# A trunk step of two layers: where the final norm is applied, and who stores its output

## The chip, the cores and the metric

The kernel runs on one core of one Trainium2 chip. The time is the device time in microseconds (us). All times in the profile are us from the start of the span unless marked ns. The engines are TensorE (PE; its weight loads are PEld), VectorE (DVE), ScalarE (ACT), GpSimd (POOL) and SyncE (SP, which only issues DMAs here).

## The reference

One inference step of a decoder trunk of depth 2, width 1024, float32, for 512 prompt tokens and 8 x 4 sample tokens (32). Each layer is an attention and mLSTM mixer with an output projection, then a convolutional feed-forward part with a down projection, each added to the residual stream. At the end stands the final norm, which is what the change touches:

```
def rmsnorm(x, g):
    xf = x.astype(F32)
    y = xf * lax.rsqrt(jnp.mean(xf * xf, axis=-1, keepdims=True) + EPS)
    return (y * g.astype(F32)).astype(x.dtype)
...
    y_prompt = rmsnorm(xp, final_g)
    y_sample = rmsnorm(xs, final_g)
```

## The kernel before

Activations are kept transposed: `xT` is [128 partitions, 8 chunks, 544 tokens], the width of 1024 being split into eight chunks of 128 (`KC` = 8). The tokens are 512 prompt ones (`SEQ`) and 32 sample ones (`TS`), 544 (`TT`) in all. Big products are made of three products of rounded parts each (line 1237 for the up projection, line 1263 for the down projection).

The instructions of each engine stand in one block, in program order, and the engines are tied by semaphores alone. There is no planner: the order is written out by hand. In the last down projection (`down(2, NG, last=True)`, lines 1251 to 1279) TensorE makes chunk 0 to 7 of the output, 12 matmul pairs each. VectorE adds each chunk to the residual stream (`residual`, lines 2259 to 2270; the last instruction, line 2270, signals `y_add`). ScalarE squares the chunk (line 1332) into one of two halves of `sq`. Two chunks later TensorE sums the squares over the partitions (`norm_sum`, lines 638 to 646): four matmuls with a 128x32 block of ones, each for a quarter of the 544 tokens (136), put the sums of quarter q in partitions 32q to 32q+31 of one PSUM bank. Between the chunks TensorE also turns the last rows of the convolution history (`tail_rows`, line 1248), which ScalarE copies (line 1663) and GpSimd stores (lines 2515 and 2516).

After chunk 7 the norm is finished in this order. VectorE adds epsilon (line 1695), ScalarE takes the root (line 1337), VectorE inverts 136 columns (line 1697), TensorE spreads the four quarters over all partitions (`spread`, lines 648 to 654), ScalarE copies the part of the sample tokens (line 1339). VectorE makes `xnT`: the sample tokens by two products (lines 2381 and 2383) and the prompt tokens by eight `scaled` (line 1703), each a chunk times the gain times the spread inverse root. TensorE then transposes `xnT` back to rows of tokens in ten tiles of 128 tokens by 512 columns (32 tokens in the last two), four transposes each, into four PSUM banks in turn (lines 1311 to 1320). The first half of a row needs chunks 0 to 3, the second chunks 4 to 7. ScalarE copies each tile to `ybuf` (lines 1670 to 1673), and GpSimd stores it (lines 2520 to 2526).

SyncE's queue carries only loads; its last ones are the last rows of the down weights (line 628), long before this point. GpSimd's queue carries all stores. `in_norm(S, m, k)` is the k-th increment of semaphore S in norm number m; the final norm is m = 4.

Of the kernel before, what the change touches and what calls it, by code (L numbers as in the profile page):

```python
# [13 lines left out]
D = 1024  # L14
SEQ = 512
# [110 lines left out]
def trunk_program(nc, A, O):  # L126
# [10 lines left out]
    with ctx:  # L137
# [213 lines left out]
        final_tr, final_copy = sig("final_transposed", 10), sig("final_copied", 10)  # L351
# [167 lines left out]
        def _(sp):  # L519
# [22 lines left out]
            for L in range(DEPTH):  # L542
# [6 lines left out]
                def load(stage, i, copies, j=0):  # L549

                    s = i % NSLAB
                    sp.wait_ge(slab_out[s], L * uses[s] + j + (first_use[stage, s] + i // NSLAB) + 1)
                    for dst, src in copies:
                        sp.dma_start(dst, src).then_inc(slab_in[s], 16)
# [73 lines left out]
                load("ffn", 16, down_copies(lambda k: slice(4 * NG + k, 4 * NG + k + 1), 1))  # L628


        @block.tensor
        def _(pe):
# [72 lines left out]
            for L in range(DEPTH):  # L705
# [544 lines left out]

                def down(n_k, g=0, last=False):
# [4 lines left out]
                    for c in range(8):  # L1256
# [11 lines left out]
                        if last:  # L1268
                            if c == 0:
                                pe.wait_ge(y_add.sem, y_add.at(8 * g, L))  # L1270
                            if c < 6:
                                tail_rows(c)
                            if c >= 2:
                                norm_sum(2 * L + 2, c - 2)
                    pe.drain().then_inc(slab_out[1], 1)
                    if last:
                        norm_sum(2 * L + 2, KC - 2)
                        norm_sum(2 * L + 2, KC - 1)
                        spread(2 * L + 2)
# [30 lines left out]

            for n in range(10):
                t, hf = n // 2, n % 2
                M = 128 if t < 4 else TS
                if n < 2:
                    pe.wait_ge(n_dve.sem, in_norm(n_dve, 2 * DEPTH, 4 * hf + 6))
                if n >= 4:
                    pe.wait_ge(final_copy.sem, final_copy.at(n - 3))
                for k in range(4):
                    ins = tr(ps[n % 4][0:M, 128 * k:128 * k + 128], xnT[:, 4 * hf + k, 128 * t:128 * t + M], ident)
                ins.then_inc(final_tr.sem, 1)  # L1320

        @block.scalar
        def _(act):
# [54 lines left out]
            for L in range(DEPTH):  # L1378
# [289 lines left out]
                root(2 * L + 2)  # L1668

            for n in range(10):  # L1670
                M = 128 if n < 8 else TS
                act.wait_ge(final_tr.sem, final_tr.at(n + 1))
                A_(ybuf[0:M, n, :], ps[n % 4][0:M, :], ACT.Copy).then_inc(final_copy.sem, 1)


        @block.vector
        def _(dve):
# [91 lines left out]
            for L in range(DEPTH):  # L1769
# [606 lines left out]
                inverse_root(2 * L + 2)  # L2376

            m = 2 * DEPTH
            dve.wait_ge(n_act.sem, in_norm(n_act, m, KC + 2))
            d = xnT[:, :, SEQ:TT]  # L2380
            tt(d, xT[:, :, SEQ:TT], bc(rd, 1, KC), ALU.mult)
            drain()
            tt(d, d, bc(colsB[:, 88:96], 2, TS), ALU.mult)
            drain()
            for k in range(KC):
                scaled(m, k, colsB[:, 88 + k:89 + k])
# [3 lines left out]
        def _(pool):  # L2390
# [35 lines left out]
            for L in range(DEPTH):  # L2426
# [86 lines left out]
                decode_scaled(2 * L + 1, 24)  # L2513
                pool.wait_ge(ul_c.sem, ul_c.at(6, L))
# [5 lines left out]
            for n in range(10):  # L2520
                t, hf = n // 2, n % 2
                pool.wait_ge(final_copy.sem, final_copy.at(n + 1))
                dst = y_p[0, 128 * t:128 * t + 128, 512 * hf:512 * hf + 512] if t < 4 else \
                    y_s.rearrange("b t d -> (b t) d")[:, 512 * hf:512 * hf + 512]
                pool.dma_start(dst, ybuf[0:128 if t < 4 else TS, n, :]).then_inc(stored, 16)
            pool.wait_ge(stored, DEPTH * ST_ALL + 160)
# [31 lines left out]
```

## Time and profile before

| | |
|---|---|
| median of 3 runs | 1839.16 us (1837.89 to 1844.75) |
| profiled execution | 1831.91 us |
| its span | 1830.1 us |
| instructions in the span | 37052 |
| TensorE busy | 1698.8 us, 93% |
| VectorE busy | 919.4 us, 50% |
| ScalarE busy | 610.7 us, 33% |
| GpSimd busy | 187.5 us, 10% |
| mean granted TensorE clock | 0.950 |

The span runs from the first to the last instruction of the profiled execution. A granted clock of 1.00 is 2.4 GHz, of 0.50 1.2 GHz. Busy shares are means over the span; the stretch that the change touches is the last 45 us or so, and is read from its own rows.

### The profile page before, as it was taken

To read this page: it belongs to the slowest core of one execution; us is meant where nothing else is said; L and a number is where in the kernel's file an instruction comes from. 1 tells how busy PE (TensorE), PEld (TensorE's weight loads), DVE (VectorE), ACT (ScalarE), POOL (GpSimd) and SP (SyncE) were. 2 spreads that over 40 slices of the span, in tenths; PEclk is the share of its full clock that TensorE was granted. 3 is DMA by queue.
4 is the path that set the end of the run, shared out by engine and by line. 5 is a ranking of instruction groups with operands and counts; after the bars stand their busy time and mean duration, and the time that the engine had idled before them with its cause. 6 is when DMAs were issued, how large, how long until landed. Compare 5 with 4: busy or idle time off the path is not lost.

```text
span 1830.1 us, 37052 instructions
## 1 busy us (share of the span) xinstructions
PE 1698.8 (93%) x14719; PEld 1526.7 (83%) x14719; DVE 919.4 (50%) x2374; ACT 610.7 (33%) x1165; POOL 187.5 (10%) x304
## 2 busy tenths in 40 slices
PE   5899998977989999999989999898798999999996
PEld 4799965545989999999989997645598999999995
DVE  2534434646365645546463343474545554654644
ACT  2332225634142323323152212463333332422413
POOL 1001003432000000000000100153200000000001
PEclk9899988988989999999999997898898999999998
DMA  8335278369322222221133535634861222221201
GB/s 297 118 99 181 78 273 261 115 225 200 82 76 65 92 93 93 93 92 47 49 89 90 179 102 186 221 105 137 217 114 47 92 93 93 93 92 47 93 24 54
DMA packets 157903, 219.42 MB, mean 120 GB/s; under 512 B 11722, under 2 KB 116490, under 8 KB 157548
## 3 DMA queue, kind: packets, MB, share of 16 engines
q1 hardware_dynamic: 150096, 199.22, 34.7%
q0 software_dynamic: 7648, 17.94, 3.9%
q8 instruction: 116, 1.90, 0.4%
q14 instruction: 43, 0.35, 0.1%
HBM read 200.45 MB, written 16.68 MB: 119 GB/s over the span
## 4 chain that ended last, share of the span: by engine, by line
PE 85%; DVE 5%; ACT 3%; SPq 2%; issue 2%; DMA 1%; POOL 1%; DVEq 1%; ACTq 0%
PE ps L1237 28%; PE ps L1263 15%; PE ps L809 13%; PE ps L1197 6%; PE ps L683 2%; PE ps L920 2%; PE ps L935 2%; PE ps L854 2%; PE ps L890 1%; PE ps L795 1%; PE ps L804 1%; PE ps L803 1%; SPq L546 1%; PE ps L1217 1%; PE ps L870 1%
## 5 line engine op out<-in xcount | busy, mean ns | idle before, releaser
L1237 PE MATMUL ps<-work_r,big_r 128*128 128x272 f32 x1344 | 279.2, 289 | 1.4 <-ACT work L1622 0.3
L1237 PE MATMUL ps<-work_r,slab_r 128*128 128x272 f32 x1344 | 278.5, 288 | 0.0
L1237 PE MATMUL ps<-xnT_r,big_r 128*128 128x272 f32 x1344 | 276.4, 287 | 0.0
L1237 PEld LDWEIGHTS ps<-work_r,big_r 128*128 128x128 f32 x1344 | 210.2, 188 | 3.9 <-issue 3.9
L809 PE MATMUL ps<-slab_r,work_r 128*128 128x256 f32 (+1 forms) x976 | 213.3, 285 | 0.0
L1237 PEld LDWEIGHTS ps<-xnT_r,big_r 128*128 128x128 f32 x1344 | 211.7, 188 | 0.0
L1237 PEld LDWEIGHTS ps<-work_r,slab_r 128*128 128x128 f32 x1344 | 210.5, 188 | 0.0
L1727 DVE TENSOR_TENSOR slab_r<-slab,big_r 128x2048 fp32r<-128x2048 f32 (+1 forms) x84 | 170.2, 2036 | 49.5 <-ACT big_r L1606 44.1
L809 PEld LDWEIGHTS ps<-slab_r,work_r 128*128 128x128 f32 x976 | 163.4, 191 | 2.7 <-issue 2.5
L1625 ACT ACTIVATE big<-big,work 128x560 f32<-128x560 f32 x44 | 33.7, 765 | 372.1 <-DVE big L2321 372.1
L1263 PE MATMUL ps<-side_r,big_r 128*128 128x272 f32 x704 | 148.3, 292 | 4.9 <-DVE big_r L1727 4.9
L1263 PE MATMUL ps<-big_r 128*128 128x272 f32 x704 | 146.3, 289 | 0.0
L1263 PE MATMUL ps<-side_r,slab_r 128*128 128x272 f32 x704 | 145.9, 289 | 0.0
L2265 DVE TENSOR_TENSOR work<-ps,modT 128x32 f32<-128x32 f32 x112 | 21.5, 192 | 241.6 <-PE ps L1263 181.2
L2431 POOL DMA_DIRECT2D out<-work x32 | 18.3, 578 | 1064.8 <-ACT work L1663 810.9
L1263 PEld LDWEIGHTS ps<-side_r,big_r 128*128 128x128 f32 x704 | 111.0, 190 | 7.7 <-DVE big_r L1727 5.4
L1263 PEld LDWEIGHTS ps<-big_r 128*128 128x128 f32 x704 | 111.5, 190 | 0.0
L1263 PEld LDWEIGHTS ps<-side_r,slab_r 128*128 128x128 f32 x704 | 111.0, 190 | 0.0
L1606 ACT ACTIVATE big_r<-slab 128x2048 fp32r<-128x2048 f32 x44 | 84.3, 1916 | 48.4 <-PE ps L1237 48.4
L809 PE MATMUL ps<-work_r 128*128 128x256 f32 (+1 forms) x336 | 96.3, 287 | 0.0
L809 PE MATMUL ps<-work_r,xnT_r 128*128 128x256 f32 (+1 forms) x336 | 94.1, 280 | 0.0
L809 PE MATMUL ps<-slab_r,xnT_r 128*128 128x256 f32 x320 | 90.8, 284 | 0.0
(446 smaller groups left out, 3204.9 us busy)
## 6 DMA issues: line engine op xcount, KB each, us to landing
slab<-in_w_mod SPq DMA_DIRECT2D x23, 2048.0 KB, 9.0
slab<-in_w_up SPq DMA_DIRECT2D x44, 1024.0 KB, 7.5
slab<-in_w_in SPq DMA_DIRECT2D x20, 1024.0 KB, 5.9
slab<-in_w_down SPq DMA_DIRECT2D x20, 1024.0 KB, 6.0
slab<-in_cache_cmp_kv SPq DMA_DIRECT2D x128, 128.0 KB, 2.0
slab<-in_cache_sel_kv SPq DMA_DIRECT2D x96, 128.0 KB, 2.0
big<-in_cache_win_kv SPq DMA_DIRECT2D x16, 512.0 KB, 5.2
out<-big POOLq DMA_DIRECT2D x16, 448.0 KB
```

The lines of the kernel that those rows point to most:

```text
L683: ins = mm(bank[32 * q:32 * q + 32, 0:128], cT[:, k, :], wv[:, k, 128 * q:128 * q + 128], start=k == 0, stop=k == KC - 1, tile_position=(0 ...
L809: ins = mm(ps[n % 4][:, 0:cw], x, fr(wt[:, k, :]), start=k == 0 and m == 0, stop=k == KC - 1 and m == 2)
L854: mm(ps[2 * (s % 2) + k][:, 0:nk], proj[h_, t, 128 * g:128 * g + 128], proj[h_, 0:t + 1, c:c + 128], start=True, stop=True).then_inc(a_s.s ...
L920: ins = tr(ps[4 + k][:, 128 * i:128 * i + 128], Pq[u % 6][:, 128 * i:128 * i + 128], ident)
L935: ins = mm(ps[6][64 * k:64 * k + 64, 128 * i:SEQ], proj[:, i, c + 64 * k:c + 64 * k + 64], PT[:, n % 2, k, 512 * i:384 * i + SEQ], start=b ...
L1197: ins = mm(ps[2 * (c % 3) + b][:, 0:HALF], wt, fr(x[:, k, HALF * b:HALF * b + HALF]), start=k == 0 and n == 0, stop=k == KC - 1 and n == 2)
L1237: ins = mm(ps[2 * half + b][:, 0:HALF], wt, fr(x[:, k, HALF * b:HALF * b + HALF]), start=k == 0 and n == 0, stop=k == KC - 1 and n == 2)
L1263: ins = mm(ps[bank + b][:, 0:HALF], wt, fr(x[:, k, HALF * b:HALF * b + HALF]), start=k == 0 and n == 0, stop=k == n_k - 1 and n == 2)
L1606: A_(fr(hiU[:, q % 2, :, :, :]), src[:, :, :, cc:cc + 128], ACT.Copy).then_inc(w_hi.sem, 1)
L1625: A_(cv[:, s, 0:UPW - 2], cv[:, s, 0:UPW - 2], ACT.Silu, bias=cbias[:, s:s + 1]).then_inc(u_si.sem, 1)
L1727: return tt(fr(dst), dst, fr(hi).bitcast(F), ALU.subtract)
L2265: tt(tmp.rearrange("p (b t) -> p b t", b=NB), hi[:, SEQ - HALF:HALF].rearrange("p (b t) -> p b t", b=NB), bc(gs, 2, NT), ALU.mult)
```

## The change

The final norm is no longer applied ahead of the transposes. The gain is applied first: GpSimd multiplies chunks 0 to 5 with their column of the gain as each is added, ScalarE chunks 6 and 7 after its last square. The inverse root is applied when a transposed tile is copied out of PSUM, where a token is a partition and its factor a scalar of the partition. For that the sums of squares are made for blocks of 128 tokens (`token_sums`) and turned into columns by two transposes (`token_columns`); ScalarE takes the root of five columns and VectorE inverts them. The tiles are in another order (all first halves, then all second halves) and in other banks; the first is transposed between chunks 6 and 7, and three more before the last sums. VectorE copies the even tiles and ScalarE the odd ones. SyncE stores them in place of GpSimd. The norms inside the layers stay as they were.

```diff
+        FINAL = [(n % 5, n // 5, b) for n, b in enumerate((7, 4, 5, 0, 1, 2, 3, 7, 4, 5))]
+        y_out = ctx.enter_context(nc.semaphore("final_stored"))
...
         @block.sync
+            for n, (t, hf, _) in enumerate(FINAL):
+                if n % 2:
+                    sp.wait_ge(final_copy.sem, final_copy.at(n // 2 + 1))
+                else:
+                    sp.wait_ge(n_dve.sem, in_norm(n_dve, 2 * DEPTH, 3 + n // 2))
+                cols = slice(512 * hf, 512 * hf + 512)
+                if t < 4:
+                    sp.dma_start(y_p[0, 128 * t:128 * t + 128, cols], ybuf[:, n, :]).then_inc(y_out, 16)
+                else:
+                    sp.dma_start(y_s.rearrange("b t d -> (b t) d")[:, cols], ybuf[0:TS, n, :]).then_inc(y_out, 16)
+            sp.wait_ge(y_out, 160)
...
         @block.tensor
+                def token_sums(k):
+                    pe.wait_ge(n_act.sem, in_norm(n_act, 2 * DEPTH, k + 1))
+                    for q in range(4):
+                        mm(ps[6][32 * q:32 * q + 32, 0:128], ones[:, 0:32], sq[:, k % 2, 128 * q:128 * q + 128], start=k == 0,
+                           stop=k == KC - 1, tile_position=(0, 32 * q), skip_group_check=True)
+                    mm(ps[6][0:TS, 128:128 + TS], ones[:, 0:TS], sq[:, k % 2, SEQ:TT], start=False, stop=k == KC - 1,
+                       tile_position=(0, 0), skip_group_check=True).then_inc(n_pe.sem, 1)
+
+                def token_columns():
+                    pe.wait_ge(n_dve.sem, in_norm(n_dve, 2 * DEPTH, 1))
+                    tr(ps[6][:, 256:384], rstd[:, 0:128], ident)
+                    tr(ps[6][0:TS, 384:384 + TS], rstd[0:TS, 128:128 + TS], idn(TS)).then_inc(n_pe.sem, 1)
+
+                def final_tile(n):
+                    t, hf, bank = FINAL[n]
+                    M = 128 if t < 4 else TS
+                    pe.wait_ge(n_pool.sem, in_norm(n_pool, 2 * DEPTH, (4, 6)[hf]))
+                    if hf:
+                        pe.wait_ge(n_act.sem, in_norm(n_act, 2 * DEPTH, KC + 2))
+                    if n == 7:
+                        pe.wait_ge(n_dve.sem, in_norm(n_dve, 2 * DEPTH, 3))
+                    if n == 8:
+                        pe.wait_ge(final_copy.sem, final_copy.at(1))
+                    if n == 9:
+                        pe.wait_ge(n_dve.sem, in_norm(n_dve, 2 * DEPTH, 4))
+                    for k in range(4):
+                        ins = tr(ps[bank][0:M, 128 * k:128 * k + 128], xnT[:, 4 * hf + k, 128 * t:128 * t + M], ident)
+                    ins.then_inc(final_tr.sem, 1)
...
-                            if c >= 2:
+                            if c >= 2 and L + 1 < DEPTH:
                                 norm_sum(2 * L + 2, c - 2)
+                            elif c >= 2:
+                                token_sums(c - 2)
+                            if c == 6 and L + 1 == DEPTH:
+                                final_tile(0)
                     pe.drain().then_inc(slab_out[1], 1)
-                    if last:
+                    if last and L + 1 == DEPTH:
+                        pe.wait_ge(ul_c.sem, ul_c.at(6, L))
+                        token_sums(KC - 2)
+                        final_tile(1)
+                        final_tile(2)
+                        pe.wait_ge(y_add.sem, y_add.at(8 * g + 7, L))
+                        final_tile(3)
+                        token_sums(KC - 1)
+                        final_tile(4)
+                        token_columns()
+                        pe.wait_ge(y_add.sem, y_add.at(8 * g + 8, L))
+                        for n in range(5, 10):
+                            final_tile(n)
+                    elif last:
...
         @block.scalar
+                    if L + 1 == DEPTH and c == KC - 1:
+                        for k in (KC - 2, KC - 1):
+                            A_(xnT[:, k, :], xT[:, k, :], ACT.Copy, scale=colsB[:, 88 + k:89 + k]).then_inc(n_act.sem, 1)
...
+            act.wait_ge(n_pe.sem, in_norm(n_pe, 2 * DEPTH, KC + 1))
+            A_(rstd[:, 160:164], ps[6][:, 256:384].rearrange("p (t n) -> p t n", t=4)[:, :, 0], ACT.Sqrt)
+            A_(rstd[0:TS, 164:165], ps[6][0:TS, 384:385], ACT.Sqrt).then_inc(n_act.sem, 1)
+            act.wait_ge(n_dve.sem, in_norm(n_dve, 2 * DEPTH, 2))
+            for n, (t, hf, bank) in enumerate(FINAL):
+                if n % 2:
+                    act.wait_ge(final_tr.sem, final_tr.at(n + 1))
+                    r = slice(0, 128) if t < 4 else slice(0, TS)
+                    A_(ybuf[r, n, :], ps[bank][r, :], ACT.Copy, scale=rstd[r, 160 + t:161 + t]).then_inc(final_copy.sem, 1)
...
         @block.vector
-            dve.wait_ge(n_act.sem, in_norm(n_act, m, KC + 2))
-            d = xnT[:, :, SEQ:TT]
-            tt(d, xT[:, :, SEQ:TT], bc(rd, 1, KC), ALU.mult)
-            drain()
-            tt(d, d, bc(colsB[:, 88:96], 2, TS), ALU.mult)
-            drain()
-            for k in range(KC):
-                scaled(m, k, colsB[:, 88 + k:89 + k])
+            dve.wait_ge(n_pe.sem, in_norm(n_pe, m, KC))
+            ts_(rstd[:, 0:128], ps[6][:, 0:128], 1.0 / D, EPS, ALU.mult, ALU.add)
+            ts_(rstd[0:TS, 128:128 + TS], ps[6][0:TS, 128:128 + TS], 1.0 / D, EPS, ALU.mult, ALU.add).then_inc(n_dve.sem, 1)
+            dve.wait_ge(n_act.sem, in_norm(n_act, m, KC + 3))
+            V.reciprocal(rstd[:, 160:164], rstd[:, 160:164])
+            V.reciprocal(rstd[0:TS, 164:165], rstd[0:TS, 164:165]).then_inc(n_dve.sem, 1)
             drain()
+            for n, (t, hf, bank) in enumerate(FINAL):
+                if n % 2 == 0:
+                    dve.wait_ge(final_tr.sem, final_tr.at(n + 1))
+                    r = slice(0, 128) if t < 4 else slice(0, TS)
+                    ts_(ybuf[r, n, :], ps[bank][r, :], rstd[r, 160 + t:161 + t], None, ALU.mult).then_inc(n_dve.sem, 1)
...
         @block.gpsimd
+                if L + 1 == DEPTH:
+                    for c in range(KC - 2):
+                        pool.wait_ge(y_add.sem, y_add.at(8 * NG + c + 1, L))
+                        nc.gpsimd.tensor_scalar(xnT[:, c, :], xT[:, c, :], colsB[:, 88 + c:89 + c], 1.0, ALU.mult,
+                                                ALU.mult).then_inc(n_pool.sem, 1)
                 pool.wait_ge(ul_c.sem, ul_c.at(6, L))
                 put(p_conv[L].rearrange("o j f -> (o j) f"), ulrow[0:2, :])
                 put(s_conv[L].rearrange("b j f -> (b j) f"), ulrow[2:18, :])
```

The old loops of final transposes, copies and stores (lines 1311 to 1320, 1670 to 1673, 2520 to 2525) go, and so do `root`, `inverse_root` and `spread` for the final norm.

## Rows read from the trace of the kernel before

**Rows 1.** The page, part 4: the chain that ended last, by engine.

```profile
PE 85%; DVE 5%; ACT 3%; SPq 2%; issue 2%; DMA 1%; POOL 1%; DVEq 1%; ACTq 0%
```

**Rows 2.** Chain of waits, 1775 to 1831, in time order: start, length, what.

```profile
1798.98 0.44 PE ps L1248 x4
...
1804.13 1.72 PE ps L1263 x12
...
1807.15 0.67 ACT big L1332
...
1807.86 0.48 PE ps L642 x8
...
1811.27 0.18 PE ps L654 x2
...
1818.11 3.69 PE ps L1319 x16
```

**Rows 3.** Timeline of VectorE there: start, length, instruction, idle before and its releaser.

```profile
1790.32 0.19 DVE L2270 TENSOR_TENSOR xT<-xT,work 128x32 f32<-128x32 f32 x1
...
1806.92 0.19 DVE L2270 TENSOR_TENSOR xT<-xT,work 128x32 f32<-128x32 f32 x1
1808.36 0.30 DVE L1695 TENSOR_SCALAR rstd<-ps 128x136 f32<-128x136 f32 x1 [1.25 <-PE ps L642]
1809.05 1.00 DVE L1697 RECIPROCAL rstd<-rstd 128x136 f32<-128x136 f32 x1 [0.38 <-ACT rstd L1337]
...
1812.69 5.36 DVE L1703 SCALAR_TENSOR_TENSOR xnT<-xT,colsB,ps 128x512 f32<-128x512 f32 x8
```

**Rows 4.** Timeline of ScalarE there.

```profile
1808.70 0.32 ACT L1337 ACTIVATE rstd<-rstd 128x136 f32<-128x136 f32 x1 [0.89 <-DVE rstd L1695]
...
1821.82 2.98 ACT L1673 ACTIVATE big<-ps 128x512 f32<-128x512 f32 x6 [0.25 <-PE ps L1319]
```

**Rows 5.** Timeline of GpSimd there.

```profile
1817.52 0.57 POOL L2525 DMA_DIRECT2D out<-big  x1 [14.01 <-ACT big L1673]
...
1822.71 3.15 POOL L2525 DMA_DIRECT2D out<-big  x6 [0.31 <-ACT big L1673]
```

**Rows 6.** Half microseconds: busy by engine; last come clock, DMA share, GB/s.

```profile
1766.50:1767.00 0.50, 0.50 (x6) 0.50 (x5) 0.42 (x2) 0.00 (x0) 0.00 (x0) 1.00 0.65 74
...
1811.50:1812.00 0.50, 0.00 (x0) 0.00 (x0) 0.30 (x1) 0.16 (x1) 0.00 (x0) 0.50 0.00 0
1818.50:1819.00 0.50, 0.50 (x4) 0.50 (x3) 0.00 (x0) 0.00 (x0) 0.00 (x0) 0.50 0.70 270
...
1821.50:1822.00 0.50, 0.50 (x6) 0.50 (x5) 0.00 (x0) 0.25 (x2) 0.19 (x2) 0.85 0.88 328
...
1828.00:1828.50 0.50, 0.00 (x0) 0.00 (x0) 0.00 (x0) 0.00 (x0) 0.00 (x0) 0.97 0.00 0
```

**Rows 7.** Groups, shapes kept apart: busy, mean ns of one, idle before.

```profile
L2468 POOL TENSOR_SCALAR xnT<-xnT,rstd,gates 128x512 f32<-128x512 f32 x20 | 15.2, 772 | 3.1 <-DVE rstd L2024 3.1
...
L2453 POOL TENSOR_TENSOR big<-big,rows_bc 128x2048 f32<-128x2048 f32 x2 | 9.1, 4547 | 121.1 <-ACT big L1423 121.1
...
L2097 DVE COPY work<-ps 128x512 f32<-128x512 f32 x24 | 16.6, 691 | 21.0 <-PE ps L1033 20.8
```

**Rows 8.** Timeline of SyncE's DMA issues.

```profile
136.52 8.72 SPq L547 DMA_DIRECT2D slab<-in_cache_cmp_kv  x8
...
380.40 1.76 SPq L599 DMA_DIRECT2D big<-in_cache_win_kv  x4
...
1765.93 0.83 SPq L554 DMA_DIRECT2D slab<-in_w_down  x2
```

**Rows 9.** Stretches of 4 us while modulation weights are loaded, as rows 6.

```profile
226.00:230.00 4.00, 3.89 (x21) 2.65 (x22) 3.71 (x9) 1.41 (x2) 0.96 (x1) 1.00 0.89 286
230.00:234.00 4.00, 2.62 (x7) 1.35 (x5) 2.12 (x5) 2.71 (x11) 0.00 (x0) 0.63 1.05 393
```

**Rows 10.** Timeline of TensorE in the tail.

```profile
1815.47 1.12 PE L1319 MATMUL ps<-shape_constants,xnT 128*128 128x128 f32 x4 [4.04 <-DVE xnT L1703]
```

More of the change, by code:

```diff
@@ L350, in trunk_program @@
         c_in = ctx.enter_context(nc.semaphore("conditions_and_pages_loaded"))
-        final_tr, final_copy = sig("final_transposed", 10), sig("final_copied", 10)
+        final_tr, final_copy = sig("final_transposed", 10), sig("final_copied_act", 5)
+        FINAL = [(n % 5, n // 5, b) for n, b in enumerate((7, 4, 5, 0, 1, 2, 3, 7, 4, 5))]
+        y_out = ctx.enter_context(nc.semaphore("final_stored"))
         stored = ctx.enter_context(nc.semaphore("outputs_stored"))
@@ L1309, in _ @@
                 down(2, NG, last=True)
[L1311 to L1320, printed above, removed]
         @block.scalar
@@ L1667, in _ @@
                         split_in(0, L + 1)
[L1668 to L1673, printed above, removed]
+                    if L + 1 == DEPTH and c == KC - 1:
+                        for k in (KC - 2, KC - 1):
+                            A_(xnT[:, k, :], xT[:, k, :], ACT.Copy, scale=colsB[:, 88 + k:89 + k]).then_inc(n_act.sem, 1)
+                if L + 1 < DEPTH:
+                    root(2 * L + 2)
+            act.wait_ge(n_pe.sem, in_norm(n_pe, 2 * DEPTH, KC + 1))
[7 more added lines that the diff above has]
+                    A_(ybuf[r, n, :], ps[bank][r, :], ACT.Copy, scale=rstd[r, 160 + t:161 + t]).then_inc(final_copy.sem, 1)
         @block.vector
@@ L2375, in _ @@
                 add_y(NG, 0)
-                inverse_root(2 * L + 2)
+                if L + 1 < DEPTH:
+                    inverse_root(2 * L + 2)
             m = 2 * DEPTH
-            dve.wait_ge(n_act.sem, in_norm(n_act, m, KC + 2))
-            d = xnT[:, :, SEQ:TT]
-            tt(d, xT[:, :, SEQ:TT], bc(rd, 1, KC), ALU.mult)
-            drain()
-            tt(d, d, bc(colsB[:, 88:96], 2, TS), ALU.mult)
-            drain()
-            for k in range(KC):
-                scaled(m, k, colsB[:, 88 + k:89 + k])
+            dve.wait_ge(n_pe.sem, in_norm(n_pe, m, KC))
[4 more added lines that the diff above has]
+            V.reciprocal(rstd[0:TS, 164:165], rstd[0:TS, 164:165]).then_inc(n_dve.sem, 1)
+            drain()
+            for n, (t, hf, bank) in enumerate(FINAL):
[3 more added lines that the diff above has]
+                    ts_(ybuf[r, n, :], ps[bank][r, :], rstd[r, 160 + t:161 + t], None, ALU.mult).then_inc(n_dve.sem, 1)
         @block.gpsimd
@@ L2519, in _ @@
                 assert n_st[0] == ST_ALL, (n_st[0], ST_ALL)
[L2520 to L2526, printed above, removed]
+            pool.wait_ge(stored, DEPTH * ST_ALL)
 _INS = ["x_prompt", "x_sample", "cache_cmp_kv", "cache_sel_kv", "cache_win_kv", "state_mlstm_C", "state_mlstm_n",
```

## The prediction

> **What bounds the kernel now.** I read the page's split of the chain of waits first: 85% of it is TensorE [rows 1], so over the trunk only TensorE's work counts. The change leaves the trunk alone and rewrites what follows the last down projection, so I then read the chain in order of time from there. The matmuls of chunk 7 end at 1805.85 [rows 2] and the last residual addition at 1807.11 [rows 3]. From there to the end of the span, 1830.1, are 23.0 us, and hardly any of it is matmul work: square 0.67 and sums 0.48 [rows 2], variance 0.30, a 1.00 reciprocal over 136 columns [rows 3], the spread over the partitions, decode products, eight scalings in 5.36 [rows 3], transposes (16 of them in 3.69 [rows 2]), ScalarE's copies, ten stores in turn on GpSimd's queue [rows 4, 5], and their landing. Every step waits for the one before. TensorE's granted clock falls to 0.50 (1.2 GHz) in this tail, with TensorE idle for up to 4.04 at a stretch, and comes back to 1.00 (2.4 GHz) between 1821.5 and 1822 [rows 6, 10]. The tail is a latency chain and then a store phase, and the change rewrites both.
>
> **The change part by part**, on the profile's own clock (span 1830.1, execution 1831.91, so 1.8 lie around the span).
>
> *Delay ahead of the last addition.* In chunks 2 to 7 each sum of squares becomes four 128-column matmuls and one 32-column one in place of four 136-column ones. An f32 matmul is two records in the trace, so eight become 8 + 2. The two extra cost between nothing and 0.18, the price of the spread's two 32-column records [rows 2], which load full-width weights; the eight cost 0.48, 0.06 each [rows 2], and each becomes narrower. I take 0.06 in all, the nearer row being the same operation's, six times: 0.35 (bounds 0 and 1.1). After chunk 6's matmuls TensorE also transposes the first final tile, ahead of chunk 7's. Four transposes cost 0.44 where the clock is full and 3.69/4 = 0.92 where it is half [rows 2]; here it is full: 0.44. Together the last addition moves by 0.8, to 1807.9.
>
> That tile waits for GpSimd's fourth scaling, and chunk 7's matmuls stand behind the wait. GpSimd took 0.77 for such an operation on 128x512 and 4.55 for a product of two tensors of 2048 columns [rows 7], so 128x544 is 0.8, at most 1.2. The additions that release it end from 1790.51 on, 2.37 apart in the mean [rows 3], so it keeps pace; the fourth is scaled near 1798.5, and TensorE asks near 1804.5. The wait costs nothing below some 3.4 an operation, and all six scalings lie beside matmuls. Behind them on GpSimd are the last two convolution-state stores, which move back by about 1; nothing reads them and they land before the final stores begin.
>
> *The norm.* From the addition at 1807.9: square with its hop 0.7, to 1808.6. TensorE meanwhile does chunk 6's sums and three tiles (0.45 + 3 x 0.44 after 1806.65) and is just free; chunk 7's sums to 1809.15. VectorE's variance is two operations, 0.30 [rows 3] and 0.2 for the small one: 1809.65; the fifth tile hides in that. Two transposes make it columns, 0.25: 1809.9. ScalarE takes two small roots, each under the 0.32 of the root over 136 columns [rows 4], overlapping: 0.35, to 1810.25. Ahead of them it has the scalings of chunks 6 and 7, as wide as its square, so 0.67 each [rows 2], from 1808.6: done by 1809.95, with the columns. No table is loaded for the root, as none is before the one at 1808.70 [rows 4]. VectorE inverts 128x4 and 32x1, each like its smallest operation, 0.19 [rows 3]: 0.3 overlapping, to 1810.55 (bound above 1.0, the old reciprocal). So the long reciprocal, the spread, the decode products and the eight scalings go, and from last addition to inverse it is 2.65.
>
> *Evictions and the last five tiles.* Five tiles lie in PSUM by then; the others are transposed from 1809.9 at 0.44, paced by banks that come free, until about 1813. VectorE evicts even tiles in 0.69 [rows 7], ScalarE odd ones in 0.50 (six in 2.98 [rows 4]) with the multiplication inside, side by side. The first tile is ready at 1811.25, the last near 1814. What is late next is the stores.
>
> *Stores.* They move from GpSimd, 3.15/6 = 0.53 an issue [rows 5], to SyncE. SyncE issued 512 KB of window rows in 0.44 (four in 1.76), but eight pages in 8.72, whose issues carry a register load each [rows 8]. Ours have constant addresses like the former: 0.44, so the ten take 4.4 and do not bind. From issue to first data a load on this queue took 1.0 (issued at 1765.93, data between 1766.5 and 1767 [rows 6, 8]), and so did a GpSimd store (1817.52, data after 1818.5 [rows 5, 6]). Data flow from 1812.3. The output is 544 rows of 1024 f32, 2.23 MB. On this queue loads ran at 286 to 393 GB/s when many were under way [rows 9]; the old stores made 328 in a busy half microsecond [rows 6]. Bounds 7.8 and 5.7; I take 360 GB/s, between the rows, 6.2: 1818.5. From the last data, 1828.0, to the end of the span took 2.1 [rows 6]. New end 1820.6: 9.5 less.
>
> Two rules of the Trainium skill speak to this, and no number above uses them. "TensorE: Matmul & The Clock Gate", Part 4 on PE-mode transpose, says the full clock does not engage for transposes, since they don't count as busy. This trace shows the opposite: from 1818.11 TensorE runs nothing but transposes [rows 2], and the clock rises to 1.00 within them [rows 6]. By the row it stays full in the new tail; by the rule the last tiles run at half, 0.92 each, and the sum is some 0.5 worse. "DMA: Bandwidth & Descriptors", Latency and other measured facts, puts a hardware queue's first byte 0.4 ahead of GpSimd's; the rows show 1.0 for both, and by the rule the sum would be 0.4 better.
>
> The median of the runs shown is 1839.16, 7.3 above the profiled execution. I take the saving off it: 1839.16 - 9.5 = 1829.7.
>
> **The rivals.**
> 1. *SyncE's issues pace the stores.* For it: eight page issues in 8.72 [rows 8]. Against: the 0.44 of the window loads beside them. At 1.05 the tenth issue starts at 1811.3 + 9.5 = 1820.8 and the span ends 1.0 + 0.2 + 2.1 later, 1824.1: saving 6.0, time 1833.2. A store rate of 286 costs 1.6 more than the forecast and joins this case.
> 2. *The clock falls in the new tail.* For it: it fell by 1811.5 in the old one [rows 6]. Against: there TensorE had little to do, here tiles fill its waits. Columns and three last tiles at half cost 0.3 + 0.7: 1830.7.
> 3. *Nothing of the delay shows:* extra matmuls are free and stores run at 393 GB/s: 0.35 + 0.5 more saved, 1828.8.
> 4. *Slower.* No store stands on SyncE's queue anywhere in the trace, only loads. If 2 KB rows written from it ran slowly, the store phase would give all back. It breaks even where 2.23 MB take 6.2 + 9.5 = 15.7, 142 GB/s; at 85 GB/s they take 26.2, and the time is 1849.7. For it: only that it is unseen. Against: loads of this queue run as fast as GpSimd's stores did [rows 6, 9].
>
> **How the numbers follow.** Forecast 0.51 (own range 1828.0 to 1831.5), rival 1 0.24, rival 2 0.10, rival 3 0.12, rival 4 0.03. A measurement of this kernel tells a change of about 0.5%, 9.2 us, from none. The forecast is on that edge: 0.33 of its 0.51 lies beyond it, and with rival 3 and a little of the others faster has 0.48. Slower is rival 4, 0.03; the rest, 0.49, is within 0.5%. The range goes from rival 3 less 2.3 (the three runs of before spread over 6.9, so a median may move by some 2) to rival 1 plus 1.8: 1826.5 to 1835.0.
>
> **What would show it.** The last residual's end some 0.8 later; the inverse 2.65 after it; evictions on both engines in step; SyncE's ten issues at 0.44; data without gaps for about 6.2; the granted clock at 1.00 until TensorE's last transpose; a span of 1820.6. I am wrong if issues are 1.0 apart, if the data phase passes 7.8, or if chunk 7's matmuls wait for GpSimd.

## The result and the profile after

The changed kernel takes 1826.05 us (median of 8 runs, 1823.34 to 1831.08). The kernel before, run again beside it, has a median of 1836.38 over its now 8 runs (1829.23 to 1844.75). The ratio is 0.9941, 95% interval 0.9923 to 0.9960: 10.3 us less by the medians. A second set of runs on one chip gave 1826.89 against 1836.98, ratio 0.9943 (0.9927 to 0.9960). The forecast was a saving of 9.5 us and a time of 1829.7, range 1826.5 to 1835.0. The measured time lies 0.45 us under the range.

The page of the changed kernel, its span and part 4:

```profile
span 1824.0 us, 37076 instructions
...
PE 86%; DVE 4%; ACT 3%; SPq 2%; issue 2%; DMA 1%; POOL 1%; DVEq 1%; ACTq 0%
```

The share of TensorE in the chain [rows 1] is up a point, as the tail around it is shorter. The chain of waits of the changed kernel from chunk 6 on (start, length, what), against [rows 2]:

```profile
1806.68 1.70 PE ps L1309 x12
1808.38 0.35 PE ps L1269 x8
1808.73 0.04 PE ps L1271 x2
1808.77 0.59 PE ps L1294 x4
1809.36 1.50 PE ps L1309 x12
...
1811.26 0.27 issue
...
1811.97 1.46 PE ps L1294 x12
1813.43 0.36 PE ps L1269 x8
...
1815.36 2.71 DVE big L2452 x4
```

The timeline of VectorE. Its first line is the start of the product for the last chunk of the hidden layer of the feed-forward part; its second line answers to the last addition in [rows 3], the 0.18 and the 0.12 to the reciprocal of 1.00 there:

```profile
1790.46 0.44 DVE L2390 TENSOR_TENSOR big<-ps,big 128x272 f32<-128x272 f32 x1 [2.89 <-PE ps L1251]
...
1811.95 0.19 DVE L2331 TENSOR_TENSOR xT<-xT,work 128x32 f32<-128x32 f32 x1
1813.87 0.29 DVE L2442 TENSOR_SCALAR rstd<-ps 128x128 f32<-128x128 f32 x1 [1.72 <-PE ps L1271]
...
1815.04 0.18 DVE L2445 RECIPROCAL rstd<-rstd 128x4 f32<-128x4 f32 x1 [0.80 <-ACT rstd L1728]
1815.14 0.12 DVE L2446 RECIPROCAL rstd<-rstd 32x1 f32<-32x1 f32 x1
1815.35 3.37 DVE L2452 TENSOR_SCALAR big<-ps,rstd 128x512 f32<-128x512 f32 x5
```

ScalarE and GpSimd in the same stretch (the last square, the two scalings, the five copies; and the fourth of GpSimd's scalings):

```profile
1812.18 0.66 ACT L1384 ACTIVATE big<-xT 128x544 f32<-128x544 f32 x1 [1.83 <-DVE xT L2331]
1812.74 1.37 ACT L1722 ACTIVATE xnT<-xT,colsB 128x544 f32<-128x544 f32 x2
...
1815.29 3.17 ACT L1734 ACTIVATE big<-ps,rstd 128x512 f32<-128x512 f32 x5 [0.28 <-DVE rstd L2446]
```

```profile
1802.37 0.72 POOL L2583 TENSOR_SCALAR xnT<-xT,colsB 128x544 f32<-128x544 f32 x1 [1.82 <-DVE xT L2331]
```

SyncE's ten final issues, in place of GpSimd's [rows 5]:

```profile
1816.13 1.81 SPq L639 DMA_DIRECT2D out<-big  x4
1817.99 0.55 SPq L641 DMA_DIRECT2D out<-big  x1
1818.58 2.29 SPq L639 DMA_DIRECT2D out<-big  x4
1820.91 0.67 SPq L641 DMA_DIRECT2D out<-big  x1
```

Half microseconds of the changed kernel, with the columns of [rows 6]:

```profile
1816.50:1817.00 0.50, 0.50 (x7) 0.50 (x6) 0.50 (x2) 0.50 (x2) 0.00 (x0) 1.00 0.06 25
1817.00:1817.50 0.50, 0.50 (x7) 0.43 (x5) 0.50 (x2) 0.50 (x2) 0.00 (x0) 1.00 1.01 377
...
1820.50:1821.00 0.50, 0.00 (x0) 0.00 (x0) 0.00 (x0) 0.00 (x0) 0.00 (x0) 1.00 1.05 397
...
1822.50:1823.00 0.50, 0.00 (x0) 0.00 (x0) 0.00 (x0) 0.00 (x0) 0.00 (x0) 0.50 1.00 320
1823.00:1823.50 0.50, 0.00 (x0) 0.00 (x0) 0.00 (x0) 0.00 (x0) 0.00 (x0) 0.50 0.18 62
1823.50:1824.00 0.50, 0.00 (x0) 0.00 (x0) 0.00 (x0) 0.00 (x0) 0.00 (x0) 0.50 0.00 0
```

I measure the tail from the end of the last residual addition to the end of the span, because it doesn't move with what the trunk did before: 1807.11 to 1830.1 is 23.0 before, 1812.14 to 1824.0 is 11.9 after. So the tail lost 11.1 us. Read in the same four pieces as the prediction, whose values for the kernel before come from half microseconds:

| piece | before | predicted | after |
|---|---|---|---|
| last addition to first store's issue | 10.4 | 3.4 | 4.0 |
| issue to first data | 1.0 | 1.0 | 0.8 |
| first to last data | 9.5 | 6.2 | 6.3 |
| last data to end of the span | 2.1 | 2.1 | 0.8 |

Data fill the DMA engines without a gap from 1817.0 to 1823.0, at shares of 0.92 to 1.07. Nine of these twelve half microseconds have 365 to 397 GB/s, three have 275 to 320. The last data are seen at 1823.2. TensorE's last transpose ends at 1817.75, and the granted clock is still 1.00 in the slice from 1820.5; that from 1822.5 has 0.50.

The spans of the two profiled executions differ by only 6.1, though the tail alone is 11.1 shorter. The rest is the trunk. VectorE's product for the last hidden chunk starts at 1784.40 in the profile of before and at 1790.46 in this one, with the same instructions ahead of it.

### The profile page after: what moved, and what is told of

It reads as the page before. It is cut to its first block, busy times and chain, and to the rows that moved or that the text cites. A ratio compares the mean times of both kernels' runs of the same rounds, so it can differ in the third digit from the quotient of the medians.

```text
span 1824.0 us, 37076 instructions
## 1 busy us (share of the span) xinstructions
PE 1700.2 (93%) x14727; PEld 1528.8 (84%) x14727; DVE 916.1 (50%) x2371; ACT 609.5 (33%) x1162; POOL 185.6 (10%) x300
## 4 chain that ended last, share of the span: by engine, by line
PE 86%; DVE 4%; ACT 3%; SPq 2%; issue 2%; DMA 1%; POOL 1%; DVEq 1%; ACTq 0%
PE ps L1251 28%; PE ps L1309 15%; PE ps L823 13%; PE ps L1211 6%; PE ps L697 3%; PE ps L934 2%; PE ps L949 2%; PE ps L868 2%; PE ps L1231 2%; PE ps L904 1%; PE ps L809 1%; PE ps L818 1%; SPq L548 1%; PE ps L817 1%; DMA work<-in_x_sample 1%
```

## The experiments

All numbers below are tails as defined above, read from each kernel's own profile; the ratio is of timed runs to the kernel before. "To the addition" is the time from the start of VectorE's last hidden product (first line of the VectorE fence above) to the end of the last addition.

| kernel | tail | to the addition | ratio (95%) |
|---|---|---|---|
| before | 22.99 | 22.71 | 1 |
| changed | 11.86 | 21.68 | 0.9941 (0.9923 to 0.9960) |
| changed, again | 11.88 | 23.23 | 0.9943 (0.9927 to 0.9960) |
| gpsimd_stores | 14.60 | 23.24 | 0.9971 (0.9951 to 0.9992) |
| scalar_copies | 11.72 | 23.25 | 0.9939 (0.9918 to 0.9960) |
| both_undone | 14.15 | 23.25 | 0.9951 (0.9933 to 0.9970) |
| before_sync_stores | 20.91 | 22.73 | 0.9996 (0.9981 to 1.0012) |
| before_kept_busy | 25.75 | 21.17 | 1.0018 (1.0000 to 1.0036) |
| before_kept_busy_short | 22.13 | 22.73 | 0.9984 (0.9969 to 0.9999) |
| gpsimd_all_eight | 11.87 | 23.26 | 0.9941 (0.9923 to 0.9958) |
| sums_first | 11.48 | 23.24 | 0.9932 (0.9908 to 0.9956) |
| tile_behind | 11.54 | 22.85 | 0.9932 (0.9900 to 0.9964) |
| drain_last | 11.38 | 21.28 | 0.9925 (0.9906 to 0.9944) |
| half_stored | 10.27 | 23.26 | one run |

Two profiles of the changed kernel have tails of 11.86 and 11.88, and the span is shown to 0.1 us, so with SyncE's stores a tail tells a change of 0.1 to 0.2 us, where the timed ratio tells some 3 us. No kernel with GpSimd's stores was profiled twice; a difference of a few tenths between those is less sure.

### What of the change is worth what

**Stores back on GpSimd.**

```diff
-            for n, (t, hf, _) in enumerate(FINAL):      # in block.sync
...
+            for n, (t, hf, _) in enumerate(FINAL):      # at the end of block.gpsimd
+                ...
+                    pool.dma_start(y_p[0, 128 * t:128 * t + 128, cols], ybuf[:, n, :]).then_inc(y_out, 16)
```

> The changed kernel with the ten final stores back on GpSimd's queue, nothing else. I read the tail: from the end of the last residual addition to the end of the span, 23.0 us before, 11.9 after. Theory A: ten stores of 2.23 MB are bound by the DMA engines (share 1.0, some 380 GB/s) on either queue, and SyncE's queue only ends sooner (0.9 from last data to the end of the span after, 2.1 before): tail 13.1, i.e. +1.2. Rival B: the queue sets the store rate itself; GpSimd's stores had half microseconds at 0.47 to 0.7 of share before, so the data phase goes from 6.2 to 7.5 or more: tail 14.5 or more. Rival C: the queue is worth nothing, tail 11.9.

Measured: tail 14.60, 2.7 more than the changed kernel. Theory A's 13.1 falls and rival B's tail holds, though the data phase is 7.3 and not 7.5 or more. The sooner end that theory A named is in the 2.7 as well. GpSimd's first issues and half microseconds:

```profile
1819.25 2.17 POOL L2587 DMA_DIRECT2D out<-big  x4 [7.18 <-DVE big L2441]
```

```profile
1820.00:1820.50 0.50, 0.50 (x6) 0.29 (x3) 0.50 (x2) 0.50 (x1) 0.50 (x2) 1.00 0.27 106
...
1821.00:1821.50 0.50, 0.00 (x0) 0.00 (x0) 0.50 (x1) 0.32 (x1) 0.50 (x2) 1.00 0.61 213
...
1823.50:1824.00 0.50, 0.00 (x0) 0.00 (x0) 0.00 (x0) 0.00 (x0) 0.50 (x2) 0.50 0.86 205
...
1827.50:1828.00 0.50, 0.00 (x0) 0.00 (x0) 0.00 (x0) 0.00 (x0) 0.00 (x0) 0.50 0.05 16
```

The first issue comes 4.25 after the last addition (4.0 on SyncE), the first data 1.1 after it, the data end near 1827.7, 7.3 later (6.3 on SyncE), and the span 1.9 after that (0.8). Before 1826.5 the share is 0.61, 0.78 and twice 0.86 in four slices, where the changed kernel never falls under 0.92. So the queue counts at four places: 0.25, 0.25, 1.1 and 1.1.

**Copies by ScalarE alone.**

```diff
-                if n % 2:
+                if True:                                 # ScalarE copies all ten tiles
                     act.wait_ge(final_tr.sem, final_tr.at(n + 1))
...
-            for n, (t, hf, bank) in enumerate(FINAL):    # VectorE's copies
```

> The changed kernel with all ten copies out of PSUM on ScalarE, none on VectorE. Theory A (stores bound the end): ScalarE delivers a tile per 0.63, the DMA engines take 0.68 for one, so the last data move by under 0.3 and the tail stays 11.9 to 12.3. Rival B (copies bound the end once one engine makes them): ten copies at 0.63 plus a hop each for tiles 7 to 9, that now wait for a bank, end 3 us later and the tail is 13 or more.

Measured: tail 11.72, 0.14 less. ScalarE's copies, and the end of the data:

```profile
1817.73 5.81 ACT L1727 ACTIVATE big<-ps,rstd 128x512 f32<-128x512 f32 x10 [0.28 <-DVE rstd L2439]
```

```profile
1825.00:1825.50 0.50, 0.00 (x0) 0.00 (x0) 0.00 (x0) 0.00 (x0) 0.00 (x0) 0.50 0.78 234
1825.50:1826.00 0.50, 0.00 (x0) 0.00 (x0) 0.00 (x0) 0.00 (x0) 0.00 (x0) 0.50 0.00 0
```

Ten copies take 5.81, 0.58 apart, where ScalarE's five beside VectorE's are 0.63 apart, and the first store can go at 1818.45, 3.87 after the addition instead of 4.0. The tail lies 0.2 under theory A's range, but its mechanism holds and rival B falls: the stores take 6.2 and hide the copies. Sharing the copies between two engines, part of the change, gave nothing here.

**Both undone.** The edits of the two above together.

> The changed kernel with both undone: copies by ScalarE alone and stores on GpSimd's queue. What is left of the change is the norm behind the transposes with its gain by GpSimd. Theory A: the two add up to +1.2 to +1.6, tail 13.1 to 13.5; then 9.5 of the 11.1 us that the tail lost belong to the reordered norm. Rival B: the rest is worth under half, tail 17 or more.

```profile
1806.56 0.19 DVE L2316 TENSOR_TENSOR xT<-xT,work 128x32 f32<-128x32 f32 x1
```

Measured: the span is 1820.9, so the tail is 14.15. That is 0.65 over theory A's range, whose store term was 1.2 where gpsimd_stores has 2.7. Its main point stands: with GpSimd's stores and one copying engine the reordered norm brings the tail from 22.99 to 14.15, 8.8 of the 11.1 us. These 8.8 include the new order of the tiles and the clock that stays up; no run separates them. With the stores on GpSimd, ScalarE alone is 0.45 faster than the pair (14.15 against 14.60): the first issue comes 0.12 sooner and the data phase is some 6.9 in place of 7.3. Why it gains more there than the 0.14 with SyncE's stores stays open.

**Only the stores moved, in the kernel before.**

```diff
-                pool.wait_ge(final_copy.sem, final_copy.at(n + 1))
+                sp.wait_ge(final_copy.sem, final_copy.at(n + 1))
...
-                pool.dma_start(dst, ybuf[0:128 if t < 4 else TS, n, :]).then_inc(stored, 16)
+                sp.dma_start(dst, ybuf[0:128 if t < 4 else TS, n, :]).then_inc(y_out, 16)
```

> The kernel before with its ten final stores on SyncE's queue, nothing else. Theory A: the old tail is paced by transposes and ScalarE's copies up to 1824.8, so the queue gives only its sooner end, -1.2, and little by shorter issues: tail 21.4 to 22.0. Rival B: the queue's rate counts: tail 20.5 or less. Rival C: nothing, 23.0.

Measured: tail 20.91, 2.1 less. That is 0.5 under theory A's range and 0.4 over rival B's, so neither holds as stated; the timed ratio, 0.9996 (0.9981 to 1.0012), can't tell 2 us from nothing. The last copy ends 17.7 after the addition in both kernels. The last data come 2.1 after that copy in place of 3.1, and the span ends 1.1 after them in place of 2.2, both read in slices of 0.1 us. So the queue is worth 2.1 in the old order and 2.7 behind the reordered norm.

**GpSimd scaling all eight chunks.**

```diff
-                    for c in range(KC - 2):
+                    for c in range(KC):
...
-                        for k in (KC - 2, KC - 1):       # ScalarE's two scalings
-                            A_(xnT[:, k, :], xT[:, k, :], ACT.Copy, scale=colsB[:, 88 + k:89 + k]).then_inc(n_act.sem, 1)
```

> The changed kernel with GpSimd scaling all eight chunks and ScalarE none. Theory A: ScalarE's two scalings (1.37, ending 1814.11) are off the path, its roots wait for TensorE's columns until 1814.80; GpSimd would end chunk 7 at 0.75 after the last addition. The tail stays 11.9 within 0.2. Rival B: TensorE's second-half tiles wait for ScalarE's scalings now, and the tail shortens by 0.5 or more.

Measured: tail 11.87. Theory A holds, ScalarE's two scalings are hidden as the prediction had them.

### The clock in the old tail

```diff
+                def busy(n):
+                    for _ in range(n):
+                        mm(ps[4][:, 0:128], ident, ident, start=True, stop=True)
...
+                            busy(12)                     # 5 in the second kernel
                         spread(2 * L + 2)
+                            busy(30)                     # 13
...
+                if n == 0:
+                    busy(12)                             # 5
```

> The kernel before with 12 + 30 + 12 extra 128-column matmuls of the unit matrix into an unused bank, placed where TensorE idles in the tail (before the spread, behind it, behind the first tile). Theory A: the fall of the granted clock to 0.50 costs the old tail real time: its 16 chained transposes took 3.69 at half clock and would take 1.8 at full, so the tail goes from 23.0 to about 21, and that much of the change's gain is the clock. Rival B: the copies pace anyway and the clock is worth under 0.5: tail 22.5 or more. If clock does not stay up with transposes and such matmuls, the granted clock shows 0.50 there as before.

This one was mis-sized: a matmul is two records, and the extra ones ran longer than the idle stretches they were to fill.

```profile
1817.56 2.95 PE L1254 MATMUL ps<-shape_constants 128*128 128x128 f32 x24
...
1821.41 6.95 PE L1254 MATMUL ps<-shape_constants 128*128 128x128 f32 x60
```

The tail grew to 25.75, which prices my mistake and not the clock. It does show the granted clock at 1.00 from the last addition, through this work, to the last transpose at 1835.4. With the right count:

> As before_kept_busy, but 5 + 13 + 5 extra matmuls of two records each of 0.11, to fit TensorE's idle stretches of 1.8, 4.0 and 1.5 (the 12 + 30 + 12 of before were 2.95, 6.95 and 2.84 long and delayed the tail by 2.8). Theory A: with the clock at 1.00 the 16 chained transposes take 1.8 in place of 3.69 and the copies come 0.50 apart in place of 0.86; the stores then bind: tail 21.0 to 21.8. Rival B: stores on GpSimd's queue had no room to begin with, tail 22.5 to 23.0.

```profile
1824.36 4.42 ACT L1685 ACTIVATE big<-ps 128x512 f32<-128x512 f32 x9 [2.04 <-PE ps L1329]
```

```profile
1824.50:1825.00 0.50, 0.50 (x7) 0.50 (x6) 0.00 (x0) 0.50 (x2) 0.00 (x0) 1.00 0.01 0
...
1831.00:1831.50 0.50, 0.00 (x0) 0.00 (x0) 0.00 (x0) 0.00 (x0) 0.00 (x0) 0.56 0.94 320
...
1832.50:1833.00 0.50, 0.00 (x0) 0.00 (x0) 0.00 (x0) 0.00 (x0) 0.00 (x0) 0.50 0.09 33
```

Nine copies take 4.42, 0.49 apart, where at half clock they came 0.85 apart until the clock rose (the last six in 2.98 [rows 4]). The last copy ends 16.1 after the last addition, against 17.7 before. The extra matmuls delay nothing ahead of the tiles: VectorE's first of eight scalings starts 5.58 after the addition in both kernels. But the tail is 22.13, only 0.9 less, between the two theories: GpSimd's store phase takes back 0.7. So of what the old tail took, the half clock was 0.9 us, by one profile of each kernel.

### The order behind chunk 7

The changed kernel's square of chunk 7 ends at 1812.84, its sums start at 1813.43: TensorE is behind, with the sums of chunks 5 and 6, 0.27 of waiting and three tiles (1.46) queued ahead.

```diff
                         final_tile(2)
-                        pe.wait_ge(y_add.sem, y_add.at(8 * g + 7, L))
-                        final_tile(3)
                         token_sums(KC - 1)
-                        final_tile(4)
+                        pe.wait_ge(y_add.sem, y_add.at(8 * g + 8, L))
+                        final_tile(3)
                         token_columns()
-                        pe.wait_ge(y_add.sem, y_add.at(8 * g + 8, L))
+                        final_tile(4)
```

> The changed kernel with TensorE's order behind chunk 7 altered: sums of chunk 7 ahead of the third final tile, and the columns ahead of the fourth (in the changed kernel the square of chunk 7 ends at 1812.84, 0.70 after the last addition, but its sums start at 1813.36, since three tiles stand before them). Theory A: the norm chain is what releases copies and stores, so every 0.1 of it shows: sums 0.45 earlier, columns 0.45 earlier, tail 11.4. Rival B: the store phase has slack elsewhere (tiles not ready, issues), and the tail stays 11.9.

Measured: 11.48, 0.4 less. Theory A holds.

The next kernel also moves the first tile. Its edit against the changed kernel:

```diff
-                            if c == 6 and L + 1 == DEPTH:
-                                final_tile(0)
...
                         token_sums(KC - 2)
+                        final_tile(0)
                         final_tile(1)
+                        token_sums(KC - 1)
                         final_tile(2)
-                        pe.wait_ge(y_add.sem, y_add.at(8 * g + 7, L))
-                        final_tile(3)
-                        token_sums(KC - 1)
-                        final_tile(4)
                         token_columns()
                         pe.wait_ge(y_add.sem, y_add.at(8 * g + 8, L))
+                        final_tile(3)
+                        final_tile(4)
```

> As sums_first, and the first final tile is moved from between chunks 6 and 7 to behind chunk 7. Behind chunk 7 stand now: sums of chunks 5 and 6, two tiles, sums of chunk 7, one tile, columns, the rest. Theory A: the last addition comes 0.59 sooner (the chain shows 0.59 for that tile), the chain behind it is as in sums_first (square ends 0.70 after the addition, TensorE gets there at about the same time): tail 11.4 to 11.6 and the distance from the last hidden product to the end of the span 1.0 to 1.1 shorter than in the changed kernel. Rival B: too few tiles are ready when copies start, copies wait for TensorE and the gain is under 0.5.

Measured: 11.54, as theory A had it, and 22.85 in place of 23.24 to the addition: 0.7 less in all than in the changed kernel, where 1.0 to 1.1 were expected. The tile's place between the chunks had cost 0.39, not the 0.59 that the chain shows for it: the twelve pairs behind it have 1.50 there in place of 1.70, which gives 0.20 of it back. TensorE in tile_behind, behind the sums of chunk 5:

```profile
1811.53 0.42 PE L1269 MATMUL ps<-big,shape_constants 128*32 128x128 f32 x8 [0.36 <-issue]
...
1811.90 1.09 PE L1294 MATMUL ps<-shape_constants,xnT 128*128 128x128 f32 x8
1812.93 0.42 PE L1269 MATMUL ps<-big,shape_constants 128*32 128x128 f32 x8
```

The program has TensorE's drain in the 0.36 ahead of the second sums; the next kernel moves it behind the last tile (edit against tile_behind).

```diff
-                    pe.drain().then_inc(slab_out[1], 1)
+                    if not (last and L + 1 == DEPTH):
+                        pe.drain().then_inc(slab_out[1], 1)
...
                         for n in range(5, 10):
                             final_tile(n)
+                        pe.drain().then_inc(slab_out[1], 1)
```

> As tile_behind, with TensorE's drain of the last down projection moved behind the last final tile (the trace of tile_behind shows 0.36 without work there, between the sums of chunks 5 and 6). Theory A: TensorE reaches the sums of chunk 7 as the square ends; they start 0.1 earlier, tail 11.4; ratio to the kernel before 0.9935, and to the changed kernel on the same chip about 0.9995. Rival B: something else waits in that gap and the tail stays 11.5.

Measured: tail 11.38, as theory A had it, and the 0.36 is gone. TensorE now waits for ScalarE's square before the sums of chunk 7, so nothing of its own is left ahead of them:

```profile
1811.47 0.43 PE L1269 MATMUL ps<-big,shape_constants 128*32 128x128 f32 x8 [0.32 <-ACT big L1384]
```

On one chip this kernel ran at 0.9925 (0.9906 to 0.9944) of the kernel before and the changed one at 0.9943 (0.9927 to 0.9960), medians 1823.57 and 1826.89. The intervals overlap; what is shown is the 0.5 in the tail and the 0.4 to the addition, about 0.9 us.

### What binds the end

```diff
-                cols = slice(512 * hf, 512 * hf + 512)
+                cols = slice(512 * hf, 512 * hf + 256)
```

This kernel leaves out half of the final output.

> The changed kernel storing only the first 256 of the 512 columns of each final tile (half of the final output is left out). It tells what binds the end. Theory A: the DMA engines: 1.11 MB in place of 2.23, so the last data would come 3.1 sooner, tail 8.8, unless issues bind first; ten issues at 0.44 from 4.0 after the last addition end at 8.4, with 1.0 to the data and 0.75 to the end of the span 10.2 to 10.3. So issues should bind here, tail 10.2 (9.9 to 10.6). Rival B: neither data nor issues but the copies and transposes pace (last copy 6.6 after the last addition), or the end has a fixed length: tail 11.5 or more.

```profile
1815.02 1.81 SPq L639 DMA_DIRECT2D out<-big  x4
...
1819.29 0.45 SPq L641 DMA_DIRECT2D out<-big  x1
```

```profile
1817.00:1817.50 0.50, 0.00 (x0) 0.00 (x0) 0.50 (x1) 0.35 (x1) 0.00 (x0) 1.00 0.81 268
...
1820.00:1820.50 0.50, 0.00 (x0) 0.00 (x0) 0.00 (x0) 0.00 (x0) 0.00 (x0) 1.00 0.58 176
1820.50:1821.00 0.50, 0.00 (x0) 0.00 (x0) 0.00 (x0) 0.00 (x0) 0.00 (x0) 1.00 0.00 0
```

Measured: tail 10.27. Issues are 0.45 apart (0.47 in the second four), the shares in full half microseconds 0.83 and less, and the data end 1.2 after the last issue starts. Theory A holds: with half the data SyncE's issues bind, 1.6 us under what the full data need. With all the data the second four issues stretch to 0.57 (four in 2.29), at a time when the share is 1.0.

### The trunk and the median

> The changed kernel once more, unchanged, beside the kernel before on one chip. Theory A: the change saves the length that its tail lost less the delay ahead of the last addition, 11.1 - 0.5 = 10.6 us, and the missing 0.45 us of the range came from the median of three runs that the saving was taken from: ratio 0.9942 +- 0.0010, with the kernel before near 1836, not 1839. Rival B: the trunk gains or loses too: ratio outside 0.993 to 0.9955. In the profile the tail is 11.9 again, while the start of the last hidden product may lie anywhere between 1783 and 1795.

Measured: ratio 0.9943, medians 1826.89 and 1836.98, tail 11.88. Theory A holds. The start of the last hidden product, with the same instructions ahead of it in all of them, was at 1784.40 in the profile of before, 1783.50 in both_undone, 1790.46 and 1786.09 in the two of the changed kernel and 1795.28 in before_kept_busy: 11.8 us of spread before anything of the change runs.

```profile
1786.09 0.44 DVE L2390 TENSOR_TENSOR big<-ps,big 128x272 f32<-128x272 f32 x1 [2.89 <-PE ps L1251]
```

The tail of the trunk moves too. In this second profile TensorE made chunk 0 at the lower clock (1.2 GHz), in the first at the full one, which is the 1.55 between 23.23 and 21.68. A half microsecond of chunk 0 in the second profile, then a piece of two records of chunk 0 in the first, in 0.41, where the second takes 0.66:

```profile
1789.50:1790.00 0.50, 0.50 (x4) 0.50 (x4) 0.00 (x0) 0.00 (x0) 0.00 (x0) 0.50 0.15 33
```

```profile
1793.67 0.41 PE L1309 MATMUL ps<-side_r,big_r 128*128 128x272 f32 x2
```

Pairs in one clock state give the delay ahead of the last addition: 23.24 - 22.72 = 0.52 with the lower clock in chunk 0 (22.71 in before and 22.73 in before_sync_stores), 21.68 - 21.17 = 0.51 with the full one (changed kernel and before_kept_busy).

## Why the prediction was off, step by step

**The direction and the mechanism were right.** The norm's chain went, the stores became the bound, the clock stayed up. The saving by profile is 11.1 - 0.52 = 10.6 us; the medians gave 10.3, the prediction 9.5. Of the 0.3 between profile and medians, 0.1 lies around the span: the time of a run less its span is 1.9 in the changed kernel and 1.8 before, where the prediction kept 1.8.

**The step that put the time out of the range** was the last: "The median of the runs shown is 1839.16 ... I take the saving off it". Three runs were too few for a trunk that spreads by some 12 us. The kernel before has 1836.38 over 8 runs, and beside the experiments 1836.14 over 31, 1835.73 over 21 and 1836.98 over 17: the median of three was 2.2 to 3.4 high. 1839.16 less the 10.6 of the profiles would have been 1828.6, inside; 1836.38 less my 9.5 would have been 1826.9, just inside. Both errors together made the 0.45 outside. The range's lower end allowed 2.3 for a median's movement below rival 3, and nothing for an end of the span shorter than 2.1, the next point.

**The end of the span, 2.1 predicted, 0.8 measured: -1.3.** This is the mis-sized term of the sum. I carried the time from the last data to the end of the span over from stores on GpSimd's queue to stores on SyncE's without bounding it. gpsimd_stores puts it back to 1.9, so it belongs to the queue: it is 1.9 to 2.2 in all five profiles with GpSimd's stores, and 0.8 to 0.9 in eight of the nine with SyncE's (1.1 in before_sync_stores). Two sides of the same error: I said that the queue's issues do not bind and gave it nothing else, while it is worth 2.7 in all.

**The delay ahead of the last addition, 0.8 predicted, 0.52 measured: -0.3.** The two extra small matmuls cost 0.04, less the narrower ones (0.39 in place of 0.37 in a pass): 0.02 a chunk, not 0.06. They come five times ahead of the last addition and not six, as the sums of chunk 5 stand behind chunk 7's matmuls. The tile cost 0.39, for 0.44.

**From addition to first issue, 3.4 predicted, 4.0 measured: +0.6.** "TensorE is just free" when the square ends was the wrong step: I had counted the sums of chunk 6 and three tiles behind chunk 7, and left out the sums of chunk 5, which stand there too, and the drain. TensorE was 0.6 late. sums_first and drain_last recovered 0.5 of it by order alone. Inverse roots, variance and columns came as worked out: 1813.43 to 1815.26 is 1.8, predicted 1.9.

**The copies.** ScalarE's were 0.63 apart, not 0.50, and VectorE's 0.67. It made no difference, since scalar_copies shows that half of that capacity would do.

**The data phase, 6.2 predicted, 6.3 measured.** 360 GB/s between the rows was right: mostly 365 to 397 in the slices, 275 to 320 in three. half_stored shows why issues did not bind: they need 1.6 less. With the issue to first data (1.0 predicted, 0.8 measured) the pieces add up: -1.3 - 0.3 + 0.6 - 0.2 + 0.1 is -1.1, the 10.6 against the 9.5.

**GpSimd's scalings** took 0.72, not 0.8, right behind each addition, and TensorE never waited for them.

**The clock.** It stayed at 1.00 with transposes as TensorE's main work from 1811.97 on, so rival 2 did not come. The rule of the Trainium skill's "TensorE: Matmul & The Clock Gate" (Part 4, PE-mode transpose: the full clock doesn't engage for transposes) is contradicted here a second time for f32 transposes, after [rows 6]. The Trainium skill's first bytes in "DMA: Bandwidth & Descriptors" (Latency and other measured facts) had the right sign: 0.8 on SyncE's queue, 1.1 on GpSimd's in gpsimd_stores, a difference of about 0.25 where the Trainium skill has 0.4.

**The other rivals.** Rival 1 (issues 1.05 apart pace the stores) did not come: they were 0.45 to 0.57 apart, and even 0.45 binds only with half the data. Rival 4 (slow stores) did not come. Rival 3's saving, 10.35, is nearest to the measured one, though for another reason than it gave.

**The chances.** I gave 0.48 to faster by over 0.5%. The measured 0.59% is over that edge, and its interval's upper end, 0.996, is not.

## What to carry to other kernels

A scale that is one factor a token can be applied where tokens are partitions, in the copy out of PSUM that is there anyway; what lies ahead of it then needs no norm and hides beside the matmuls, and this, with the order of the tiles and the clock, was worth 8.8 of 11.1 us. Measure such a tail from the last instruction that both kernels share, since here it repeats to within 0.1 us while the runs of one kernel spread by eight and more; and take the price of a store from the queue that will issue it, its end included. When work is put ahead of a critical instruction "to fill a wait", list everything in that engine's order up to it: one forgotten 0.4 and a drain turned the wait into lateness.

## What the runs showed of the hardware

- The last ten stores cost 2.7 us more from GpSimd's queue than from SyncE's: 1.9 against 0.8 from the last data to the end of the span, 7.3 against 6.3 of data, 1.1 against 0.8 to the first data, and a first issue 0.25 later (gpsimd_stores against the changed kernel).
- Stores of 2 KB rows from SyncE's queue ran at 365 to 397 GB/s at shares of 0.98 to 1.05 in nine of twelve half microseconds of the changed kernel, near the loads' 393 GB/s at 1.05 [rows 9].
- SyncE's issues with constant addresses are 0.45 apart when the DMA engines have room (half_stored) and 0.57 when their share is 1.0 (the changed kernel).
- TensorE's granted clock rose from 0.50 to 1.00 (2.4 GHz) within transposes alone in the kernel before [rows 2, 6]. It stayed at 1.00 on transposes in the changed kernel and on matmuls of a unit matrix in before_kept_busy.
